# Third expert's rows found by a slot-matrix product; gather and bias spreads among the table stores

## The reference

```python
logits = (ht @ w_router + b_router).astype(jnp.float32)
top_val, top_idx = lax.top_k(logits, TOP_K)          # 4 of 32 experts
gates = jax.nn.softmax(top_val, axis=-1)
...
gu = xb @ w_gu + b_gu                                # rows of one expert, 1024 -> 2048
x_glu = jnp.minimum(gu[..., :D_EXPERT], SWIGLU_LIMIT)
x_lin = jnp.clip(gu[..., D_EXPERT:], -SWIGLU_LIMIT, SWIGLU_LIMIT)
act = x_glu * jax.nn.sigmoid(SWIGLU_ALPHA * x_glu) * (x_lin + 1.0)
yb = act @ w_dn + b_dn
y = jnp.zeros((T, D), h.dtype).at[rows_tok].add(yb * rows_gate[:, None])
```

## Time and profile before

| | us |
|---|---|
| median of 3 runs | 1441.19 |
| lowest and highest run | 1440.02, 1444.81 |
| the profiled execution's own time | 1441.16 |
| its span | 1439.4 |
| PE busy | 1390.4 (97% of the span) |
| DVE, ACT, POOL busy | 1248.3, 1051.0, 395.5 |
| PE share of the chain that ended last | 88% |

### The profile page before, as it was taken

One profiled execution on the slowest core, in us unless ns is written; L12 is line 12 of the kernel. 1 busy time (PEld: TensorE's weight loads), 2 busy tenths in 40 slices (PEclk: granted clock), 3 DMA queues, 4 the chain that ended last, 5 costly groups with the idle time before them and its releaser, 6 DMA issues.

```text
span 1439.4 us, 19737 instructions
## 1 busy us (share of the span) xinstructions
PE 1390.4 (97%) x6579; PEld 1155.4 (80%) x6579; DVE 1248.3 (87%) x957; ACT 1051.0 (73%) x770; POOL 395.5 (27%) x232
## 2 busy tenths in 40 slices
PE   7999999995999999999999999999999999999996
PEld 6877888874888888888888888888888888888874
DVE  5534647495999999999999999999999999999997
ACT  5234334484888888888888888888888888888873
POOL 0000001065233333333333333333333333333341
PEclk9999999997999999999999999999999999999998
DMA  8311323487899999999999999999999999999983
GB/s 318 101 59 59 103 74 121 157 306 275 313 388 381 377 376 379 380 382 378 380 377 381 376 381 375 383 382 382 383 379 379 387 380 382 384 382 378 370 335 124
DMA packets 80135, 453.73 MB, mean 315 GB/s; under 512 B 12825, under 2 KB 13089, under 8 KB 31852
## 3 DMA queue, kind: packets, MB, share of 16 engines
q1 hardware_dynamic: 68968, 432.55, 76.6%
q0 software_dynamic: 10016, 17.44, 4.8%
q10 hardware_dynamic: 1124, 3.38, 0.7%
HBM read 447.60 MB, written 22.59 MB: 327 GB/s over the span
## 4 chain that ended last, share of the span: by engine, by line
PE 88%; DMA 3%; DVE 2%; POOL 2%; ACT 2%; issue 2%; ACTq 0%; DVEq 0%; POOLq 0%
PE ps L1904 15%; PE ps L1909 15%; PE ps L1905 15%; PE ps L1862 8%; PE ps L1864 8%; PE ps L1870 8%; PE ps L1542 4%; PE ps L1550 4%; PE ps L1543 4%; PE ps L1840 2%; PE ps L1853 2%; POOL slot_table L633 2%; DMA acc_rows<-y,idx_scatter 1%; DMA slot_table<-entry,entry_at 1%; PE ps L1645 1%
## 5 line engine op out<-in xcount | busy, mean ns | idle before, releaser
L1904 PE MATMUL ps<-whi,xT_hi 128*128 128x512 f32 x992 | 389.4, 393 | 1.4 <-ACT ps L932 0.8
L1075 DVE TENSOR_TENSOR wlo<-raw,whi 128x2048 fp32r<-128x2048 f32 x144 | 329.2, 2290 | 67.0 <-ACT whi L734 66.7
L1905 PE MATMUL ps<-whi,xT_lo 128*128 128x512 f32 x992 | 386.1, 389 | 0.0
L734 ACT ACTIVATE whi<-raw 128x2048 fp32r<-128x2048 f32 x144 | 275.9, 1918 | 94.7 <-PE ps L1909 73.0
L1071 DVE SCALAR_TENSOR_TENSOR wlo<-raw,gffn,whi 128x2048 fp32r<-128x2048 f32 x124 | 313.0, 2566 | 2.5 <-ACT whi L732 1.6
L1909 PE MATMUL ps<-wlo,xT_hi 128*128 128x512 f32 x992 | 265.6, 389 | 0.0
L732 ACT ACTIVATE whi<-raw,gffn 128x2048 fp32r<-128x2048 f32 x124 | 245.2, 2002 | 10.7 <-PE ps L1909 10.0
L1904 PEld LDWEIGHTS ps<-whi,xT_hi 128*128 128x128 f32 x992 | 186.3, 188 | 40.3 <-ACT ps L932 1.2
L1909 PEld LDWEIGHTS ps<-wlo,xT_hi 128*128 128x128 f32 x992 | 186.2, 188 | 38.7
L1905 PEld LDWEIGHTS ps<-whi,xT_lo 128*128 128x128 f32 x992 | 186.3, 188 | 37.7
L1862 PE MATMUL ps<-whi,actT_hi 128*128 128x512 f32 x496 | 197.4, 398 | 0.0
(11 more groups left out here) (254 smaller groups left out, 1886.0 us busy)
## 6 DMA issues: line engine op xcount, KB each, us to landing
raw<-in_w_gate_up SPq DMA_DIRECT2D x130, 1024.0 KB, 8.6
raw<-in_w_down SPq DMA_DIRECT2D x126, 1024.0 KB, 9.1
raw_a<-in_w_gate_up SPq DMA_DIRECT2D x63, 1024.0 KB, 7.2
raw_b<-in_w_gate_up SPq DMA_DIRECT2D x63, 1024.0 KB, 7.5
raw<-in_w_in SPq DMA_DIRECT2D x14, 1024.0 KB, 5.3
raw<-in_w_out SPq DMA_DIRECT2D x4, 1024.0 KB, 4.9
x<-in_x SPq DMA_DIRECT2D x4, 512.0 KB, 7.5
acc_rows<-x SPq DMA_DIRECT2D x4, 512.0 KB, 5.0
```

What stands on the lines that cost most here:

```text
L734: nc.scalar.activation(whi_slot(n), raw_slot(slot_of(n)), ACT.Copy).then_inc(hi_done, 1)
L1075: nc.vector.tensor_tensor(wlo_slot(n), raw_slot(slot_of(n)), whi_slot(n).bitcast(F32), ALU.subtract).then_inc(lo_done, 1)
L1904: mm(ps[:, part, :], xT_hi[:, u, :], w_hi_ap, start=False, stop=False, skip_group_check=True)
L1905: mm(ps[:, part, :], xT_lo[:, u, :], w_hi_ap, start=False, stop=False, skip_group_check=True)
```

## The change

POOL's entries: after the eighth store it waits until PE has transposed expert 1's rows, and gathers expert 2's rows by `idx_first[:, 1:2]`. Four stores follow, then the two spreads of expert 2, then the last four stores, the table read, the memset, and the wait for the table. The loop's body starts with the gather of expert i+3 and ends with the spreads of expert i+3; it has one round less, and the last gather and scatter of that kind stand behind it (`move_rows(E - 3)`). DVE builds a second slot matrix (in `has`, from `pair_pos[:, c, 2:3]`) ahead of `xT0_lo`; PE multiplies it with the token numbers too (four more small matmuls, `next_rows`); ACT's one index instruction writes two columns. On ACT the first half of expert 0's tokens is copied ahead of `bias_to_gate(0)`, and `bias_to_gate(1)` ahead of `hi(28)`.

```diff
--- before.py
+++ after.py
@@ -646,33 +646,42 @@
                 store_entries(j)
             spread_gate_bias(1)
             spread_lin_bias(1)
-            for j in range(4, NC * TOPK):
+            for j in range(4, 8):
                 store_entries(j)
-            pl.wait_ge(x_tr, 1)
-            link(nc.gpsimd.memset(gate4[:, :, 3, :], 0.0))
+            pl.wait_ge(x_tr, 2)
+            pl.wait_ge(moved, 16)
+            gather_rows(idx_first[:, 1:2], moved)
+            for j in range(8, 12):
+                store_entries(j)
+            spread_gate_bias(2)
+            spread_lin_bias(2)
+            for j in range(12, NC * TOPK):
+                store_entries(j)
             pl.wait_ge(entry_out, 16 * NC * TOPK)
             pl.dma_start(tab[:, 0:E, :].rearrange("p e f -> p (e f)"),
                          slot_table.rearrange("(p e) f -> p (e f)", p=P)).then_inc(tab_in, 16)
+            pl.wait_ge(x_tr, 1)
+            link(nc.gpsimd.memset(gate4[:, :, 3, :], 0.0))
             pl.wait_ge(tab_in, 16)
-            table_index(idx_gather, 2).then_inc(gather_index, 1)
-            pl.wait_ge(x_tr, 2)
-            pl.wait_ge(moved, 16)
-            pl.wait_ge(gather_index, 1)
-            gather_rows(idx_gather[:, 0:1], moved)
             pl.wait_ge(x1_out, 16 * NC)
-            with pl.Fori(0, E - 2) as i:
-
-                spread_gate_bias(2, i)
-                spread_lin_bias(2, i)
+
+            def move_rows(i):
+
                 pl.wait_ge(x_tr, i + 3)
                 finished(moved, i * 32 + 32)
                 table_index(idx_gather, i + 3).then_inc(gather_index, 1)
-                finished(gather_index, i + 2)
+                finished(gather_index, i + 1)
                 gather_rows(idx_gather[:, 0:1], moved)
                 finished(y_s, i + 2)
                 table_index(idx_scatter, i).then_inc(scatter_index, 1)
                 finished(scatter_index, i + 1)
                 scatter_rows(moved)
+
+            with pl.Fori(0, E - 3) as i:
+                move_rows(i)
+                spread_gate_bias(3, i)
+                spread_lin_bias(3, i)
+            move_rows(E - 3)
 
             pl.wait_ge(chosen_s, 1)
             link(nc.gpsimd.tensor_tensor(prod2[:, :, :], chosen2[:, :, :],
@@ -913,10 +922,10 @@
                 nc.scalar.activation(y[:, :], ps[:, 4:6, :].rearrange("p b t -> p (b t)"), ACT.Copy,
                                      scale=tab[:, bass.ds(column, 1), 1]).then_inc(y_s, 1)
 
-            def first_index():
+            def next_indices():
 
                 act_e.wait_ge(pair_tr, 1)
-                nc.scalar.activation(idx_first[:, 0:1], ps[:, 4, 0:1], ACT.Identity,
+                nc.scalar.activation(idx_first[:, 0:2], ps[:, 4, 0:4].rearrange("p (e f) -> p e f", f=2)[:, :, 0], ACT.Identity,
                                      bias=cst[:, C_OFF:C_OFF + 1]).then_inc(idx_first_s, 1)
 
             def bias_to_gate(e, i=0):
@@ -933,18 +942,19 @@
                                      bias=cst[:, C_ONE:C_ONE + 1]).then_inc(bias_lin, 1)
 
             act_e.sem_inc(y_s, 1)
-            bias_to_gate(0)
             for g, done in ((0, half_hi), (1, x_hi)):
                 act_e.wait_ge(*((half_tr, 1) if g == 0 else (x_tr, 1)))
                 nc.scalar.activation(xT0_hi[:, 4 * g:4 * g + 4, :].rearrange("p k t -> p (k t)"), ps[:, 2 + g, :],
                                      ACT.Copy).then_inc(done, 1)
+                if g == 0:
+                    bias_to_gate(0)
             act_e.wait_ge(top_s, 1)
             nc.scalar.activation(gates[:, :, :], gates[:, :, :], ACT.Exp).then_inc(gexp_s, 1)
             act_e.wait_ge(hn_out, 16 * NC)
             act_e.dma_start(row_l[0:1, :], b_gate_up[0, 1:2, D:2 * D]).then_inc(bias_in, 16)
             hi(21)
             bias_to_lin(0)
-            first_index()
+            next_indices()
             for n in (22, 23, 24, 25):
                 hi(n)
             sigmoid(0)
@@ -953,8 +963,8 @@
             tokens_hi(1)
             act_e.wait_ge(entry_s, 1)
             act_e.dma_start(gain_row[:, :], norm_final_g.rearrange("(o d) -> o d", o=1).to_broadcast([P, D])).then_inc(fin_g_in, 16)
+            bias_to_gate(1)
             hi(28)
-            bias_to_gate(1)
             bias_to_lin(1)
             hi(29)
             with act_e.Fori(0, E - 2) as i:
@@ -1326,6 +1336,7 @@
                 last.then_inc(has_s, 1)
 
             slots_of(has1, num, lambda c: pair_pos[:, c, 1:2])
+            slots_of(has, num, lambda c: pair_pos[:, c, 2:3])
             for g, ready, done in ((0, half_hi, half_lo), (1, x_hi, x_lo)):
                 v.wait_ge(ready, 1)
                 nc.vector.tensor_tensor(xT0_lo[:, 4 * g:4 * g + 4, :].rearrange("p k t -> p (k t)"), ps[:, 2 + g, :],
@@ -1817,12 +1828,14 @@
             first_tokens(3, 0)
             first_tokens(3, 1)
 
-            def second_rows():
-
-                pe.wait_ge(has_s, 1)
+            def next_rows():
+
+                pe.wait_ge(has_s, 2)
                 pe.wait_ge(ones_s, 3)
-                for c in range(NC):
-                    last = mm(ps[:, 4, 0:2], has1[:, c, :], tok_r[:, c, :], start=(c == 0), stop=(c == NC - 1))
+                for k, of_expert in enumerate((has1, has)):
+                    for c in range(NC):
+                        last = mm(ps[:, 4, 2 * k:2 * k + 2], of_expert[:, c, :], tok_r[:, c, :], start=(k == 0 and c == 0),
+                                  stop=(c == NC - 1), skip_group_check=True)
                 last.then_inc(pair_tr, 1)
                 for c in range(NC):
                     last = mm(ps[:, 5, NC * E:NC * E + E], ones_r[:, :], masks[:, c, :], start=(c == 0), stop=(c == NC - 1))
@@ -1878,7 +1891,7 @@
                 pe.wait_ge(bias_gate, 1)
                 for u in range(U_GU):
                     if u == 1:
-                        second_rows()
+                        next_rows()
                     if u == 2:
                         pe.wait_ge(x_hi, 1)
                         pe.wait_ge(x_lo, 1)
@@ -1933,7 +1946,7 @@
             for c in range(NC):
                 last = nc.tensor.transpose(ps[:, 0, c * P:(c + 1) * P], gate4[:, c, :, :].rearrange("p g e -> p (g e)"), ident)
             last.then_inc(gate_tr, 1)
-            pe.wait_ge(has_s, 2)
+            pe.wait_ge(has_s, 3)
             for c in range(NC):
                 last = nc.tensor.transpose(ps[:, 1, c * P:(c + 1) * P], has[:, c, :].bitcast(F32), ident)
             last.then_inc(has_tr, 1)
```

## The result

| | before | after |
|---|---|---|
| median of the runs compared, us | 1440.70 (4 runs, 1440.02 to 1444.81) | 1422.06 (4 runs, 1421.38 to 1427.89) |
| the profiled execution's own time, us | 1441.16 | 1421.72 |
| its span, us | 1439.4 | 1419.9 |
| PE busy, us | 1390.4 (97%) | 1387.4 (98%) |
| PE share of the chain | 88% | 91% |

The changed kernel takes 0.9876 of the time before (95% interval 0.9854 to 0.9897), 18.6 us less in the medians, 19.4 between the two profiled executions.

A forecast was written before the change was run, and what follows sets the result against it. The prediction took PE, busy 97% of the span, as the bound, with one long stall ending with POOL's string of 16 stores. It summed 1441.16 − 17.4 (stall) + 0.8 (late table) = 1424.6 us, range 1422.0 to 1430.0.

The forecast's parts named there:

- The stall, 17.4 us: PE ahead of expert 2's tokens: 15.35 us of standing plus 2.06 us of slow clock, all taken as gone.
- The gather is in time: Expert 2's gather, issued after POOL's eighth store, has its rows there by 324 or 325, 15 us before 339.93.
- The two spreads: POOL's spreads of expert 2's biases, beside a busy DVE, take 5.6 us, to 333.4.
- The last four stores: POOL's last four table stores take 13.4 us, to 346.8, bounds 5.1 and 26.6; 10.3 us by the skill's rule alone.
- The table's cost, 0.8 us: The table lands at 357.4 against 356.6 free of charge for ACT's gated_rows of expert 0, costing 0.8 us.
- The slack, 4.4 us: ACT's gated_rows of expert 0, due at 352.2, may wait 4.4 us for the table free; each us past costs one.
- The moved spreads' cost on DVE: Spreads beside DVE units cost DVE about 0.8 us in the first round, hidden by its lead of over 4 us.
- The head: Before expert 0's units: added DVE and PE work and ACT's two order changes count 0, bounds 0 and 1.5 us.
- the pause had fed the weights: Rival: weights loaded during PE's stall; if PE then outran the loads, 9.6 us come back: 1433.4 us, chance 0.03.
- The late table: Rival: the last four stores starve; a table landing at 364 costs 7.4 us: 1431.2 us, chance 0.14.
- the slower case: Rival: table landing, at ACT's gated_rows of expert 0, from 374.0 on; landing at 379 gives 1446.2 us, chance 0.03.
- The head's rival: Rival: rows' store lands sooner or the wait at 318 shrinks, up to 1.5 us, table free: 1422.3 us, chance 0.08.

The follow-up runs named there:

- before, repeat: The kernel before, unchanged, run again and profiled a second time: 1439.4 us (1435.68 to 1443.07), ratio 0.9991.
- after, repeat: The changed kernel, unchanged, run again in more rounds and profiled a second time: 1421.74 us, ratio 0.9864.
- the reorders alone: The kernel before plus only ACT's two order changes (first token half ahead of bias_to_gate(0), bias_to_gate(1) ahead of hi(28)): 1443.15 us, ratio 1.001.
- the spreads last: The changed kernel with expert 2's two bias spreads put back behind the table's landing: 1429.71 us, ratio 0.9921.
- without the reorders, with fillers: The changed kernel with ACT's old order, plus unread matmuls: 8 ahead of expert 0's first unit, 9 ahead of the last activations: 1424.89 us, ratio 0.9893.
- after, with fillers: The changed kernel plus unread matmuls on PE: 4 ahead of expert 0's first unit, 9 ahead of the last expert's activations: 1424.51 us, ratio 0.9888.
- token half first only: The changed kernel with only bias_to_gate(1) put back behind hi(28): 1423.58 us, ratio 0.9877.
- the kernels with clears: The changed kernel with 10 or 26 unneeded clears of an idle tile on POOL ahead of the table read: 1426.42 and 1432.83 us.
- without the reorders: The changed kernel with both of ACT's order changes taken out: 1427.77 us, ratio 0.9908.
- gate biases first only: The changed kernel with only the first token half put back behind expert 0's gate biases: 1426.0 us, ratio 0.9892.
- 10 clears: The changed kernel with ten unneeded clears of the gate array on POOL ahead of the table read: 1426.42 us, ratio 0.99.

## Why the prediction was right, and where its terms were off

- **The stall, 17.4 us: right.** 15.35 us of idle time and 2.06 us of slow clock were read from the earlier trace rows; the first `y<-ps,tab` moved by 17.46 us between the two profiled executions, PE's clock is 1.00 through the place, and the rounds kept their 34.47 us. One caution came out of the repeats. From the point of 318 to the first `y<-ps,tab` it takes 51.54 us before and 34.16 after in the first pair of profiles, so 17.4; in the second pair 47.18 and 34.12, so 13.1. That the spans of the second pair still differ by 17.1 us comes from the head (2.2) and the tail (2.2), where the clock fell before and not after. The forecast had neither of these falls in its sum. A term taken from one profile can be right for it and still vary by 4 us, and that the medians came out within 2.5 us of the forecast owes something to luck.
- **The gather is in time: right.** It was issued at 315.57 as the step said; its rows were wanted at 339.90. Putting it back behind the stores took the gain away.
- **Stores nine to twelve: right**, to 327.71 (327.73 − 0.02) against 327.8. **The two spreads**: forecast 5.6 us, measured 331.62 − 0.17 − 327.73 = 3.7 in the profile and 5.9 in its repeat (327.54 to 333.48).
- **The last four stores: mis-sized.** The step took 13.4 us because one was to starve for 6.36 us as in the earlier trace rows. They took 340.98 − 331.62 = 9.4 us, and 9.3 in the repeat. The DVE timeline of the kernel after shows why:

```profile
330.18 3.28 DVE L1081 SCALAR_TENSOR_TENSOR wlo<-raw_a,gffn,whi 128x2048 fp32r<-128x2048 f32 x1
333.39 2.34 DVE L1081 SCALAR_TENSOR_TENSOR wlo<-raw_b,gffn,whi 128x2048 fp32r<-128x2048 f32 x1
335.65 6.69 DVE L1085 TENSOR_TENSOR wlo<-raw,whi 128x2048 fp32r<-128x2048 f32 x3
```

  DVE's units end near 333.4, 335.7, 337.9 and 340.1 us, and the four stores end at 334.33, 336.57, 338.77 and 340.98, each about 0.9 us behind one of these ends: one store to one unit. That is what the rule in the Trainium skill, SBUF — State Buffer, section "Who interferes with whom", would make of it; by it the prediction had worked out some 10.3 us and a table that is free. The trace agrees with the rule here, with 9.4 us measured. The store of 6.36 us, which the rule doesn't explain, is real too, but not steady. (In it three DVE units ended, not two, near 334.9, 337.1 and 339.3 us; the store ended 0.8 us behind the third.) It stood in the first profile before, in the one with the reorders alone and in the one with the spreads last, and in none of the kernel after.
- **The table's cost, 0.8 us: nothing in its place.** Forecast to land at 357.4, it landed at 350.9: 1.8 us of the difference from the spreads, 4.0 from the stores, 0.3 from landing to read, 0.4 from the read.
- **The slack, 4.4 us: nearly right.** A delay of 4.7 us cost 1.6, not 0.3. At the unit that the step named, the wait was 0.17 us, as it said. But DVE is busy for 98% of a steady round, so a lag is not caught up inside a round and meets later units, as the wait of 0.76 us at 386.99 shows.
- **The moved spreads' cost on DVE: hidden**, as said. The unit of 3.28 us in the rows above is one of those lengthened, and PE did not wait for it.
- **The head, taken as 0 with bounds 0 to 1.5 us: right in the pair, but as the sum of two terms that it had both at 0.** In the two profiled executions PE began 0.89 us sooner and reached the point of 318.02 at 317.94, so 0.08 us. Without the reorders, but at full clock thanks to fillers, the changed kernel reaches it at 319.00: its added work, held for hidden, and a later start of the first unit (292.19 against 291.61) cost 1.0 us, and the token half's place takes 1.2 us back (317.81 with both reorders and fillers, 317.84 with the token half first alone). Of the 1.0 us, 0.45 are the four more small matmuls (eight take 0.95 us where four took 0.50). The step had ACT working without a gap to the sigmoid, so that PE's part was covered. In the kernel with fillers and without reorders ACT waits for PE's units instead, and the sigmoid comes at 308.31 where it was at 307.30:

```profile
304.80 2.19 ACT L737 ACTIVATE whi<-raw,gffn 128x1024 fp32r<-128x1024 f32 x2 [0.53 <-PE ps L1885]
```

  On top of this the step did not ask what PE's clock does behind a wait, and the two profiles without a fall at the head hid that.
- **The tail, not in the sum at all: 1.67 us.** Behind a wait of about 2.2 us for the last activations (2.26 and 2.19) the clock was 0.58 before (1400 to 1404 us) and 1.00 after. No run shows that the change acts there, so as far as the prediction goes these 1.67 us are luck. The row of the kernel before:

```profile
1399.30 1.16 PE L1853 MATMUL ps<-cst,act 128*128 128x128 f32 x8 [2.26 <-DVE act L1370]
```

  The table's 0.8, these 1.67 and 0.39 at the very end make the 2.9 us by which the profiled execution came out below the forecast.
- **The rivals.** That the pause had fed the weights falls: the rounds after it are as before, and the only wait for a weight unit, 1.43 us on ACT, is hidden. The late table and the slower case did not happen, though the kernels with clears show that their mechanism works. The head's rival named 1422.3, which is near the median, but by another mechanism (an earlier store of rows and a shorter wait at 318), and that one did not happen.

**The clock, as far as the runs go.** Nine of the profiles, with the wait before the first unit, the point of 318 (where PE gets expert 1's linear biases), the last gap between two `y<-ps,tab`, and where the clock fell:

| kernel | wait, us | point of 318 | last gap | clock fell at | span |
|---|---|---|---|---|---|
| before | 2.13 | 318.02 | 38.38 | tail (and in the stall) | 1439.4 |
| before, repeat | 2.13 | 319.90 | 38.62 | head, tail (and in the stall) | 1437.1 |
| after | 1.12 | 317.94 | 36.71 | nowhere | 1419.9 |
| after, repeat | 0.92 | 317.75 | 36.45 | nowhere | 1420.0 |
| without the reorders | 2.40 | 320.59 | 39.04 | head, tail | 1426.3 |
| token half first only | 1.39 | 317.84 | 37.50 | nowhere | 1420.9 |
| gate biases first only | 1.43 | 319.36 | 36.74 | nowhere | 1422.5 |
| after, with fillers | none | 317.81 | 36.78 | behind 318 | 1423.0 |
| without the reorders, with fillers | 0.32 | 319.00 | 37.53 | nowhere | 1423.4 |

A fall at the head costs some 1.6 us: from the first unit to the point of 318 it takes 26.41 us before and 27.96 in its repeat; 26.82 without the reorders with fillers and 28.42 without fillers. So of the 6.4 us that the profile without the reorders is longer, the clock carries about 3.0 (1.6 at the head, 1.4 at the tail). The other half stays at full clock: 1.1 us at the head, 0.95 of a longer wait at the tail, and 1.4 behind the last `y<-ps,tab`. Why that last stretch varies between 31.4 and 33.1 us over these profiles, and why the wait at the tail does between 1.9 and 3.1 without fillers, is open. Nor does the length of a wait decide over a fall: at the head 2.13 us went both ways, at the tail 2.19 us did (held in the kernel after, fell with 10 clears), 2.99 us held with the token half first only, and behind the wait of 1.0 us at 318, which the kernel after and its repeat pass at full clock, the clock of the kernel with fillers fell.

## What to carry to other kernels

Where a stall hangs on a string of slow issues on one queue, look which consumer needs only part of their result and whether it can get that part in another way; then it is the place of the consumer in the queue that pays, and what stood behind it (here the bias spreads) must move with it. When PE is near 98% busy, count a wait on it of 2 us as possibly 3.5, for the clock may fall behind it. Small work added to an engine is hidden only as long as the engine that it hides behind is really the later one: here nearly all of a delay of 1.0 us showed. And take two profiles of the kernel before: from the point of 318 to the first `y<-ps,tab` they differ by 4.4 us.

## What the runs showed of the hardware

- PE's clock can fall to its lower level behind a wait of only 2.1 us: in the repeat of the kernel before it was 0.86 over the 12 us around it, with matmuls 0.43 us apart instead of 0.23, at a cost of some 1.6 us. Another execution passed the same wait at 1.00. The fastest runs of the kernel before (1436 us) have a mean granted clock of 0.992 and the slowest (1445 to 1447) one of 0.988, so falls of the clock go with its scatter; how much of it they make is not shown.
- An indirect store from POOL beside full DVE units ends about 0.9 us after a DVE unit ends, mostly the next one, so it takes 1.9 to 3.1 us instead of 0.97, but now and then only after several. In the first profile before, such a store began 1.03 us ahead of a run of three `TENSOR_TENSOR` units and took 6.36 us; in the kernel after one began 1.01 us ahead of the same run and took 1.93. What decides between them is open.
- Rows gathered beside busy DMA engines took 6.9 to 10.4 us to land in the kernel after, against 4.2 at best in the earlier trace rows, where the engines had been 0.60 busy. A table read of 32 KB took 4.1 us there and 5.95 in the repeat of the kernel before.
